# A hybrid decoder layer: the row of inverse roots through a DRAM scratch instead of products with the identity

## The reference

```
h = rms_norm(x, attn_norm)       # x * inv * gain, inv = rsqrt(mean(x*x) + 1e-6), one per token
proj = h @ w_in                  # split into q_r, k_r, v_r, g_r, q_m, k_m, v_m
qr = rotary(heads(q_r), pos)     # likewise kr; then retention on qr, kr, v_r
gates = sigmoid(h @ w_gate + b_gate)
```

## Time and profile before

| | us |
|---|---|
| median of 3 runs | 459.36 |
| the profiled execution's own time | 459.09 |
| its span | 456.8 |
| PE busy | 453.0 |
| DVE busy | 320.7 |
| ACT busy | 253.1 |
| POOL busy | 37.5 |

### The profile page before, as it was taken

One profiled execution on the slowest core, in us unless ns is written; L12 is line 12 of the kernel. 1 busy time (PEld: TensorE's weight loads), 2 busy tenths in 40 slices (PEclk: granted clock), 3 DMA queues, 4 the chain that ended last, 5 costly groups with the idle time before them and its releaser, 6 DMA issues.

```text
span 456.8 us, 7674 instructions
## 1 busy us (share of the span) xinstructions
PE 453.0 (99%) x3077; PEld 419.0 (92%) x3077; DVE 320.7 (70%) x391; ACT 253.1 (55%) x362; POOL 37.5 (8%) x41
## 2 busy tenths in 40 slices
PE   8999999999999999999999999999999999999997
PEld 6899999888888999999999888999999999988886
DVE  5689994756997649672469475898888888884423
ACT  6785354056665759234435356677676767573300
POOL 0100000353450021210000000000000000000000
DMA  8997554256798325996456354535544545447002
GB/s 283 424 416 263 207 200 169 93 202 212 189 281 281 125 93 188 290 328 209 185 185 234 135 184 184 187 122 221 210 184 184 184 184 184 185 176 285 0 0 93
DMA packets 29707, 90.88 MB, mean 199 GB/s; under 512 B 16368, under 2 KB 17264, under 8 KB 20336
## 3 DMA queue, kind: packets, MB, share of 16 engines
q1 hardware_dynamic: 29264, 88.92, 55.5%
q0 software_dynamic: 416, 1.57, 1.0%
HBM read 85.77 MB, written 1.05 MB: 190 GB/s over the span
## 4 chain that ended last, share of the span: by engine, by line
PE 98%; DMA 1%; ACT 0%; DVE 0%; SPq 0%; issue 0%
PE bank L485 18%; PE bank L483 18%; PE bank L484 18%; PE bank L438 5%; PE bank L437 5%; PE bank L439 5%; PE bank L725 4%; PE bank L726 4%; PE bank L728 4%; PE bank L631 2%; PE bank L633 2%; PE bank L632 2%; PE bank L451 2%; PE bank L461 2%; PE bank L455 2%; PE bank L504 1%
## 5 line engine op out<-in xcount | busy, mean ns | idle before, releaser
L1015 DVE TENSOR_TENSOR w_pair<-w_raw,w_pair 128x2048 fp32r<-128x2048 f32 x73 | 166.9, 2300 | 57.7 <-ACT w_pair L745 57.5
L745 ACT ACTIVATE w_pair<-w_raw 128x2048 fp32r<-128x2048 f32 x73 | 138.6, 1919 | 37.2 <-PE bank L728 17.1
L483 PE MATMUL bank<-h_hi,w_pair 128*128 128x256 f32 x512 | 143.7, 281 | 0.0
L484 PE MATMUL bank<-h_lo,w_pair 128*128 128x256 f32 x512 | 142.9, 279 | 0.0
L485 PE MATMUL bank<-h_hi,w_pair 128*128 128x256 f32 x512 | 142.9, 279 | 0.0
L484 PEld LDWEIGHTS bank<-h_lo,w_pair 128*128 128x128 f32 x512 | 96.2, 188 | 0.1
L483 PEld LDWEIGHTS bank<-h_hi,w_pair 128*128 128x128 f32 x512 | 96.2, 188 | 0.1
L485 PEld LDWEIGHTS bank<-h_hi,w_pair 128*128 128x128 f32 x512 | 96.2, 188 | 0.0
L483 PE MATMUL bank<-a_hi,w_pair 128*128 128x256 f32 x192 | 53.7, 280 | 0.0
L484 PE MATMUL bank<-a_lo,w_pair 128*128 128x256 f32 x192 | 53.6, 279 | 0.0
L485 PE MATMUL bank<-a_hi,w_pair 128*128 128x256 f32 x192 | 53.6, 279 | 0.0
(11 more groups left out here) (150 smaller groups left out, 598.6 us busy)
## 6 DMA issues: line engine op xcount, KB each, us to landing
w_raw<-weights_dram SPq DMA_DIRECT2D x73, 1024.0 KB, 5.1
w_raw<-weights_dram SPq DMA_DIRECT2D x8, 256.0 KB, 4.6
w_raw<-weights_dram SPq DMA_DIRECT2D x4, 512.0 KB, 8.7
ys<-x_dram SPq DMA_DIRECT2D x2, 512.0 KB, 8.6
xs<-x_dram POOLq DMA_DIRECT2D x1, 1024.0 KB, 5.6
area<-decay_dram SPq DMA_DIRECT2D x1, 768.0 KB, 9.0
out_dram<-ys SPq DMA_DIRECT2D x3, 256.0 KB, 2.0
xs<-x_chan_dram SPq DMA_DIRECT2D x1, 512.0 KB, 6.1
```

Of the source, the lines that this page charges most:

```text
L483: mm(o, s_hi, r_hi[:, k, :], start=(k == 0 and m % 2 == 0), stop=False)
L484: mm(o, s_hi, r_lo[:, k, :], start=False, stop=False)
L745: A(w_parts(n, r)[0], raw[r][:, :], ACT.Copy).then_inc(hi_ready, 1)
L1015: tt(lo, raw[r][:, :], hi.bitcast(f32), ALU.subtract).then_inc(lo_ready, 1)
```

## The change

The two products with the identity (four matmul records) are gone from PE, and the unit `inv_row` from the list of units. GpSimd, after the second inverse root, issues a DMA that writes `inv_x` (128 x 2 floats, 1 KB) to a scratch in DRAM, waits for it to land, and issues a second DMA that reads the 256 numbers into all 128 partitions (128 KB) of `area[:, 4096:4352]`. In DRAM the two columns lie interleaved (token p of tile 0, token p of tile 1, ...), so the row lies in SBUF with the two tiles interleaved too; DVE reads it as a view with a step of two floats, and the other operands as views cut by tile. The wait for the identity moves from `inv_rows` to `transposes`. `h_high` waits on `hn_ready` for both halves.

```
-for _name, _count in (("inv_row", 1), ("ret_scores", 4), ("ret_out", 4), ("ret_t0", 2),
+for _name, _count in (("ret_scores", 4), ("ret_out", 4), ("ret_t0", 2),
...
+        inv_row = area[:, 4096:4096 + SEQ].rearrange("p (s t) -> p t s", t=NT)
+        inv_x_dram = nc.dram_tensor("inv_x_dram", (P, NT), f32, kind="Internal").ap()
...
                 inv_sqrt(inv_x[:, t:t + 1], ss_x[:, t:t + 1], 1.0 / D, 1).then_inc(inv_x_ready, 1)
+            pool.wait_ge(inv_x_ready, NT)
+            pool.dma_start(inv_x_dram, inv_x[:, :]).then_inc(inv_x_out, 16)
+            pool.wait_ge(inv_x_out, 16)
+            pool.dma_start(area[:, 4096:4096 + SEQ], inv_x_dram.rearrange("p t -> (p t)").partition_broadcast(P)).then_inc(inv_row_loaded, 16)
...
             def transposes(name, j, pieces):
+                pe.wait_ge(ident_loaded, 16)
...
-            def inv_rows():
-
-                pe.wait_ge(ident_loaded, 16)
-                pe.wait_ge(inv_x_ready, NT)
-                o = start_unit("inv_row", 0)
-                for t in range(NT):
-                    ins = mm(o[:, P * t:P * t + P], inv_x[:, t:t + 1].broadcast_to([P, P]), ident[:, :],
-                             start=(t == 0), stop=(t == NT - 1))
-                ins.then_inc(unit_made, 1)
...
                 value_products(k)
-                if k == 6:
-                    inv_rows()
...
-                    if kh == 0:
-                        act.wait_ge(hn_ready, 1)
-                    else:
-                        wait_unit_read(act, unit("inv_row", 0))
+                    act.wait_ge(hn_ready, kh + 1)
...
-                u = unit("inv_row", 0)
-                dve.wait_ge(unit_made, u + 1)
+                dve.wait_ge(inv_row_loaded, 16)
                 dve.wait_ge(rotary_loaded, 16)
                 for table in (cos_t, sin_t):
-                    ins = tt(table, table, ubank(u)[:, 0:SEQ], ALU.mult)
+                    ins = tt(by_tile(table), by_tile(table), inv_row, ALU.mult)
...
-                    ins = stt(out=hn_t[:, k, :], in0=x_t[:, k, :], scalar=gain_col[:, k:k + 1], in1=ubank(u)[:, 0:SEQ],
+                    ins = stt(out=by_tile(hn_t[:, k, :]), in0=by_tile(x_t[:, k, :]), scalar=gain_col[:, k:k + 1], in1=inv_row,
                               op0=ALU.mult, op1=ALU.mult)
```

More of the change, by code:

```diff
@@ L184, in hybrid_layer @@
         h_ready = sem("h_ready")
+        inv_x_out = sem("inv_x_out")
+        inv_row_loaded = sem("inv_row_loaded")
         rot_ready = sem("rot_ready")
@@ L1027, in xg_low, with by_tile @@
                     op0=ALU.mult, op1=ALU.subtract).then_inc(xg_lo_ready, 1)
+            def by_tile(part):
+                return part.rearrange("p (t s) -> p t s", t=NT)
             def scale_tables():
-                u = unit("inv_row", 0)
-                dve.wait_ge(unit_made, u + 1)
+                dve.wait_ge(inv_row_loaded, 16)
                 dve.wait_ge(rotary_loaded, 16)
                 for table in (cos_t, sin_t):
-                    ins = tt(table, table, ubank(u)[:, 0:SEQ], ALU.mult)
+                    ins = tt(by_tile(table), by_tile(table), inv_row, ALU.mult)
                 step(ins)
             def normalise():
-                u = unit("inv_row", 0)
                 for k in range(KT):
-                    ins = stt(out=hn_t[:, k, :], in0=x_t[:, k, :], scalar=gain_col[:, k:k + 1], in1=ubank(u)[:, 0:SEQ],
+                    ins = stt(out=by_tile(hn_t[:, k, :]), in0=by_tile(x_t[:, k, :]), scalar=gain_col[:, k:k + 1], in1=inv_row,
                               op0=ALU.mult, op1=ALU.mult)
-                    if k == 3:
+                    if k % 4 == 3:
                         ins.then_inc(hn_ready, 1)
-                ins.then_inc(unit_read[u % 4], 1)
             def h_low():
```

## The result

The changed kernel takes 468.14 us, median of 4 runs (467.74 to 468.85), against 459.36: a ratio of 1.0193, 95% interval 1.0181 to 1.0205. I had predicted 461.4 and a range from 459.0 to 467.0. The direction is right; the loss is 8.8 us where I had forecast 2.0.

What follows compares the result with a forecast made beforehand. PE, busy 99% of the span, was taken to bound the kernel. Terms: -0.46 for PE, +0.19 wait at half 5, +2.3 late row, +2.0 us in sum; predicted 461.4 us, range 459.0 to 467.

Steps and rivals of the forecast that it cites:

- When the row lands: Step pricing GpSimd's two DMAs in series from 19.75 us among weight loads; row put at 28.75 us.
- T: Time at which the row lands in SBUF for DVE's tables; forecast 28.75 us.
- L: How late DVE starts the tables, T - 26.46, and with it half 5; forecast 2.3 us.
- half of one 1 MB load: Term for sharing DMA engines with weight loads: 1.25 us for each DMA, bounds 0 and a whole load.
- -0.27 + L: Change of the span: PE's gain at half 5, limited by its slack, plus DVE's lateness.
- Half 5 alone decided: Claim that only half 5's slack of 0.27 us matters; halves 6 and 8 have 1.04 and 1.2.
- The ten instructions: DVE's readers of the row, now from SBUF in steps of two floats; change in cost taken as 0.
- The gain capped at 0.27 us: PE sheds 0.46 us of products but waits 0.19 for DVE's remainder at half 5.
- In time, or nearly: Rival: row lands by 27.5 us, change between -0.27 and +0.8, time 459.1 to 460.2; 25%.
- Held back by DVE: Rival: DVE's remainder of half 4 delays the read to 26.5 us, L = 4.7, 463.8 us; 19%, shared with whole-load waits.
- each DMA waits for one or two whole loads: Other half of the 19% rival: waits behind 1 MB loads; two whole loads give nearly the same 463.8 us.
- SP's queue goes first: Rival: POOL's packets come only when weights let up after 33 us; L 8 to 13.5, time 467 to 473; 8%.

Runs made afterwards that it cites:

- experiment 7: Kernel before plus GpSimd's chain near 427 us, DMA engines silent: 1 KB write, 128 KB broadcast read, read of separate rows; 3.4, 3.8, 2.6 us issue to landing.
- experiment 8: Kernel before plus ACT's chain near 433 us, DMA engines silent: 1 KB write, 128 KB broadcast read, read of separate rows; 3.6, 3.6, 2.3 us issue to landing.
- experiment 13: Changed kernel with SyncE's loads of halves 6 and 7 and the tables held back until the row landed; 464.53 us, ratio 1.0109; write 5.9, read 3.8 us.
- experiment 14: Changed kernel with the DMA pair replaced by one earlier read of other numbers, inverse roots left out of the row; 459.17 us against 459.59, ratio 0.9994.
- experiment 1: Kernel before plus two write-and-read DMA pairs on GpSimd, awaited by no other engine, after the inverse roots and after the group norm's root; 459.24 us, ratio 1.0001.
- experiment 5: Kernel before plus a 1 KB write and an unchained 128 KB broadcast read issued by ACT at about 20 us; 7.5 and 7.3 us issue to landing.
- experiment 3: Changed kernel with 34 extra products on PE ahead of half 5 to fill the pause; 466.6 us, ratio 1.0159.
- experiment 4: Changed kernel with the tables and normalised x later in DVE's order, and ACT's high part of half 7 ahead of h; 461.88 us, ratio 1.0050.
- experiment 9: Kernel before plus the 1 KB write alone on GpSimd's queue at 20 us, nobody waiting; write took 7.1 us.
- experiment 10: Kernel before plus the 128 KB broadcast read alone on GpSimd's queue at 20 us, nobody waiting; read took 6.3 us.
- experiment 12: On top of experiment 4, SyncE loads decay, mask and columns after half 9 instead of behind half 7; 461.09 us, ratio 1.0035.
- experiment 6: Kernel before plus a 1 KB write and an unchained 128 KB broadcast read issued by GpSimd at about 20 us; 7.1 and 6.6 us issue to landing.

## Why the prediction was wrong

**The step that failed is "When the row lands".** It priced one DMA at 3.1 us fixed, 0.3 for the read's data, and 1.25 for the load: 4.35 and 4.65, T = 28.75, L = 2.3. Measured: 7.4 and 6.7, T = 34.96, L = 8.5.
- The fixed part was about right: 3.4 and 3.8 with silent engines (experiments 7, 8, 13).
- The term for the load was mis-sized, 1.25 us where it is 4.0 for the write and 2.9 for the read (7.4 - 3.4 and 6.7 - 3.8). I took "half of one 1 MB load" from the idea that queues take turns, with one packet of q8 as my witness. But that packet shows only that another queue gets in, not how long it had stood; nothing in the trace of before said when it was issued. The row that did carry a waiting time in this stretch, 10.1 us for the 64 KB identity, I had set aside as the far end. The truth lay between the two: 7.4 and 6.7 a hop, where my value was 4.35 and 4.65 and that row 10.1.
- POOL issued the write at 20.54, not 19.75. In the changed trace the last inverse root starts at 19.68 instead of 19.14, the run as a whole being some 0.5 us later, and 0.3 us pass idle before the issue. Another 0.3 us pass between the write's landing and the read's issue. These two make 1.1 of the 6.2 us by which T was missed, the two hops 5.1.

**What held.** The formula -0.27 + L gives 8.2 for the measured L of 8.5, and half 5 started 8.3 us later. Half 5 alone decided: no wait of PE stands behind it. The 0.3 us ahead of it, at half 4, I had not foreseen: DVE ran 0.5 us later in that execution, and PE, with 0.46 us less to do, reached half 4 before its remainder was ready. The ten instructions cost the same from SBUF in steps of two floats. The gain capped at 0.27 us is too small to be confirmed; experiment 14 (-0.4, an interval of about -0.8 to +0.2) does not contradict it. Two DMAs on GpSimd with nobody waiting cost nothing (experiment 1).

**The rivals.** "In time, or nearly" fell. "Held back by DVE" fell for these two hops. The read was issued at 28.28, after DVE's remainder had ended at 27.07, and was as slow with no such instruction running. The write was issued while DVE was at work (19.75 to 23.17), but ACT's write in experiment 5 waited as long for its first packet, and so did experiment 14's read, issued at 18.80 with DVE idle until 19.64. Experiment 1's second read is the one place where that rival still fits. The other half of it, "each DMA waits for one or two whole loads", was the nearest to what happened: 4.0 and 2.9 us are 1.6 and 1.2 loads of 2.5 us. It was priced at two loads for the pair, where nearly three were paid. "SP's queue goes first", given 8%, named the right time (467 to 473) and the right companion, the clock, which fell in the pause and cost 1.6 to 1.8 us, near the 2 I had put. Its mechanism is only half right: the write's packets did move among the weights. These are the DMA queues between 24.5 and 25 us:

```profile
q1 hardware_dynamic: 29, 0.20, 95.0%
q0 software_dynamic: 18, 0.00, 2.7%
```

The first of them came at 24.2, 3.7 us after the issue, the last at 25.1, and the landing followed at 27.9, 2.8 us later. The read's first packet came at 32.7, 4.4 us after its issue, the last at 34.6, and it landed 0.4 us after that. With silent engines (experiment 7) the write's first packet came 1.2 us after the issue and its landing 2.0 us after the last; for the read it was 1.5 and 0.3. So a hop is not shut out by the weights. Of what the load adds, nearly all of the read's and most of the write's (2.5 of 4.0 us) passes before the first packet moves. By the Trainium skill, "DMA: Bandwidth & Descriptors", section "Queues, rings and completion order", queues are served in turn, packet by packet. The overlap above agrees with it; how long the first turn is awaited, it does not tell. The same page of the Trainium skill, section "Anatomy of one DMA — SWDGE (gpsimd) path", gives a DMA of GpSimd's queue a fixed 2.0 us and its bytes at 436 GB/s, which for 128 KB makes an estimate of 2.3 us. With silent engines the read of separate rows agrees with that (2.6 us), the 1 KB write does not (3.4).

**Where the 8.8 us are**: about 7.2 from the late row, net of the products saved (experiment 3 against before), about 1.6 from the clock that fell in the pause. That the weights of half 5 land late costs nothing in the changed kernel, where DVE waits longer for the row; it shows only when the row's wait is gone (experiment 4, 2.6 us at half 8).

**Open**: by what the write holds back the weights behind it (323 against 418 GB/s, experiments 9 and 10), and why its landing trails its last packet by almost 3 us. Also why the 1 KB write, 8 bytes from each of 128 partitions, takes 3.4 us with silent engines where the last stores of the kernel, 128 KB each and also to DRAM, take 1.8. And why PE's first products run slowly in some executions (12 and 13) and not in others.

## What to carry to other kernels

Price a small DMA in series by its place: in a stretch where weights keep the DMA engines full, one hop cost 5.8 to 7.8 us here whichever engine issued it, with silent engines 2.3 to 3.8, and a bounce through DRAM is two hops. Before moving work from a full PE onto a DMA, look for the consumer's slack: here it was 0.27 us, and PE had only 0.46 to give. If such a row must come by DMA, put its consumers behind work that does not need it (this took back 6.3 of 8.8 us), and count what a pause of PE costs again in clock.

## What the runs showed of the hardware that I had not expected

- Load doubles the length of a tiny DMA: 1 KB to DRAM took 3.4 us with silent engines, 6.9 to 7.8 among weight loads, 4.5 and 5.9 when the loads ended meanwhile (experiments 1 and 13).
- ACT's queue and GpSimd's gave nearly the same times, silent (3.6, 3.6, 2.3 against 3.4, 3.8, 2.6) and loaded (7.5, 7.3 against 7.1, 6.6).
- With a 1 KB write to DRAM in between, the weights flowed at 303 to 382 GB/s from 28 to 33 us (experiments 1, 5, 6, 9); with a 128 KB read alone at 415 and 418 (14, 10), as before the change (414).
- A pause of 8.2 us took PE's clock from 1.00 to 0.50 before the pause was over, and the loss after it was 1.6 to 1.8 us. Much shorter pauses were followed by 0.50 too: 2.6 us in experiment 4 (mean clock 0.996 in two of four runs, 1.000 in the other two) and 1.9 us in 13, where half 5 then took 1.7 us longer.
